# A mixer of grouped state space and attention: in each step VectorE serves the state-space pairs ahead of the projections' and heads' part

## What is computed

```
hn = rmsnorm(x)
u, c_q, c_kv, k_pe = split(hn @ w_in)             # 1024, 512, 256, 64 columns
y_ssm = s5_group(u)                               # state space, 64 groups of 16 inputs, 64 complex states
q = rmsnorm(c_q) @ w_uq ; kv = rmsnorm(c_kv) @ w_ukv
q_pe, k_pe = rope(q_pe), rope(k_pe)
y_mla = softmax(causal(q k^T)) v                  # 8 heads
h = x + concat(rmsnorm(y_ssm), rmsnorm(y_mla)) @ w_out
```

## Time and profile before

| | us |
|---|---|
| median of three executions | 2970.51 (2969.03 to 2972.24) |
| the profiled execution, its own time | 2971.62 |
| its span in the trace | 2969.8 |
| granted clock of TensorE, mean over the span | 0.988 |
| PE busy | 2865.9 (97%) |
| DVE busy | 2034.5 (69%) |
| POOL busy | 707.5 (24%) |

### The profile page before, as it was taken

How to read it: one execution, slowest core, us unless ns; L and a number is a source line. 1 busy time by engine, 2 the same in 40 slices (tenths; PEclk the granted TensorE clock), 3 DMA queues, 4 the chain that set the end, 5 groups by cost and what they waited for, 6 DMA issues and landing times.

```text
span 2969.8 us, 52389 instructions
## 1 busy us (share of the span) xinstructions
PE 2865.9 (97%) x21098; PEld 2545.0 (86%) x21098; DVE 2034.5 (69%) x3273; ACT 1552.8 (52%) x2574; POOL 707.5 (24%) x858
## 2 busy tenths in 40 slices
PE   8989999999999999899899999998999999999998
PEld 7868988888888888788788888997888888888887
DVE  6675887765777666677777766777676665566654
ACT  7345565544555555466556655465445444444443
POOL 0342211100121220766356630001021110011112
PEclk9999999999999999999999999999999999999999
DMA  6324555556555555322222223454555555655554
GB/s 247 103 70 146 183 189 194 184 176 208 186 197 181 177 183 206 114 90 93 79 94 93 104 94 121 153 185 151 173 184 193 190 186 174 208 190 193 181 180 149
DMA packets 79823, 475.40 MB, mean 160 GB/s; under 512 B 8224, under 2 KB 11296, under 8 KB 38304
## 3 DMA queue, kind: packets, MB, share of 16 engines
q1 hardware_dynamic: 76768, 459.72, 45.1%
q10 hardware_dynamic: 2816, 12.32, 1.2%
HBM read 465.72 MB, written 6.29 MB: 159 GB/s over the span
## 4 chain that ended last, share of the span: by engine, by line
PE 81%; DVE 10%; ACT 4%; issue 3%; POOL 2%; DMA 0%; SPq 0%; ACTq 0%; POOLq 0%; DVEq 0%
PE bank L764 36%; PE bank L768 23%; PE bank L766 5%; PE bank L767 5%; PE bank L757 3%; DVE m L1295 2%; ACT m L2182 2%; POOL m L2895 1%; POOL m L2891 1%; DVE m L1341 1%; PE bank L780 1%; PE bank L1097 1%; PE bank L1208 0%; PE bank L1101 0%; DVE m L1574 0%
## 5 line engine op out<-in xcount | busy, mean ns | idle before, releaser
L768 PE MATMUL bank<-m,m 128*128 128x256 f32 x6624 | 1860.4, 281 | 0.0
L764 PE MATMUL bank<-m,m 128*128 128x512 f32 x4736 | 1649.4, 393 | 6.9 <-DVE m L2056 5.7
L1295 DVE TENSOR_TENSOR m<-m,m 128x1024 fp32r<-128x1024 f32 (+1 forms) x912 | 1029.8, 1138 | 574.4 <-ACT m L2182 568.0
L768 PEld LDWEIGHTS bank<-m,m 128*128 128x128 f32 x6624 | 1252.4, 189 | 0.2
L2182 ACT ACTIVATE m<-m 128x1024 fp32r<-128x1024 f32 (+1 forms) x912 | 877.6, 976 | 650.6 <-PE bank L768 625.9
L764 PEld LDWEIGHTS bank<-m,m 128*128 128x128 f32 x4736 | 890.4, 188 | 206.4 <-DVE m L2056 5.9
L766 PE MATMUL bank<-m,m 128*128 128x256 f32 x1888 | 562.5, 298 | 28.9 <-DVE m L1295 24.9
L767 PE MATMUL bank<-m,m 128*128 128x256 f32 x1888 | 535.0, 283 | 0.0
L766 PEld LDWEIGHTS bank<-m,m 128*128 128x128 f32 x1888 | 362.0, 192 | 49.5 <-issue 39.1
L767 PEld LDWEIGHTS bank<-m,m 128*128 128x128 f32 x1888 | 362.6, 192 | 1.3
L2871 POOL TENSOR_TENSOR m<-m,m 128x256 fp32r<-128x256 f32 x44 | 63.5, 1442 | 547.7 <-ACT m L2472 547.7
(11 more groups left out here) (372 smaller groups left out, 2824.2 us busy)
## 6 DMA issues: line engine op xcount, KB each, us to landing
m<-in_w_up SPq DMA_DIRECT2D x88, 1024.0 KB, 4.8
m<-in_w_down SPq DMA_DIRECT2D x128, 704.0 KB, 4.1
m<-in_w_gu SPq DMA_DIRECT2D x88, 1024.0 KB, 4.8
m<-in_w_out SPq DMA_DIRECT2D x48, 1024.0 KB, 5.1
m<-in_w_krv SPq DMA_DIRECT2D x48, 1024.0 KB, 4.8
m<-in_w_xbc SPq DMA_DIRECT2D x24, 1024.0 KB, 4.8
m<-in_w_z SPq DMA_DIRECT2D x16, 1024.0 KB, 4.8
m<-in_w_in SPq DMA_DIRECT2D x14, 1024.0 KB, 6.2
```

The costliest lines, as they stand in the source:

```text
L764: pe.matmul(bank.rearrange("p (a b) -> p a b", a=2), hi, x, start=kc == L.k0, stop=False)
L768: m = pe.matmul(ps, lo, x[:, 0, :], start=False, stop=last)
L1295: v.tensor_tensor(lo_of(k), raw_of(k)[0], hi_of(k).bitcast(F32), SUB).then_inc(*lo_v(("lo", k)))
```

## The change

`first_mixer` gets a flag that puts the pairs ahead of `main` in the mix. Only VectorE's program sets it; PE, ACT, POOL and SyncE keep their order. No instruction is added, taken away or resized. All lines behind the first hunk are one further down.

```
-def first_mixer(main, setup, pair, tables, output):
+def first_mixer(main, setup, pair, tables, output, pairs_lead=False):
...
-    run(mix((main, 1), (pairs, 1), (ahead, 1), (outs, 1), (setup, 1)))
+    both = [(main, 1), (pairs, 1)]
+    run(mix(*(both[::-1] if pairs_lead else both), (ahead, 1), (outs, 1), (setup, 1)))
...
                               mix((flight(head, 16, 4), 1), (timed((GATES, spaced(linear(L_glu, glu)))), 1)),
-                              paired(mla_out())), setup(), s5_pair, s5_tables, s5_output)
+                              paired(mla_out())), setup(), s5_pair, s5_tables, s5_output, pairs_lead=True)
```

## The result

| | before | after |
|---|---|---|
| median | 2968.6 us (11 executions, 2966.81 to 2972.24) | 2976.7 us (11 executions, 2972.72 to 2984.24) |
| ratio, 95% interval | | 1.0024 [1.0016, 1.0032] |
| profiled execution, its own time | 2971.62 us | 2975.61 us |
| its span | 2969.8 us | 2973.8 us |
| mean granted clock | 0.988 | 0.989 |

The change makes the kernel slower by 0.24%, some 7 us (the medians themselves lie 8.1 us apart). The forecast was 2976.5 us.

What follows compares the result with a forecast made beforehand. PE was taken to bound 130 to 140 us, then mainly a ring through DVE and POOL to 208 us. Rounds' +4.7 and the clock's +1.3 make +6.0, on the median 2970.51 giving 2976.5 us; range 2971.0 to 2979.5.

Steps and rivals of the forecast that it cites:

- Free up to 140 us: Up to pair 7: evacuations up to 3 us later and the moved c_q norm rate (2.1 us) are covered, costing nothing.
- The new wait: Pairs 8, 13 and 14 wait for `y`, queued on PE behind `main`'s work; late `y` groups given chance 0.75.
- the rival in which `y` is in time: Rounds 7 to 8, 12 to 13, 13 to 14: no late `y`, leaving +1.0, 2971.5 us; chance 0.17.
- The ring's +4.7 us: Pairs 7 to 15: the loop through DVE and POOL, with late `y`, starts pair 15 4.7 us later.
- The round into pair 10: Rope 0 with its products before the scans and two L1323 behind them: priced at 9.01 us.
- S + 2.15: From the scans' end S: a rope or the second L1323 directly behind them is done 2.15 us later.
- Four L1323 behind the scans: Before pair 8: first gets in ahead of POOL's product; all four done 2.85 us after the scans' end.
- the low bound, S + 2.25: Before pair 8: low end for finishing four L1323, from a row beside three short POOL operations at 0.77 us each.
- The clock: PE's clock falls to half rate behind a wait before `y`; counted once, +1.3 us, on top of +4.7.
- The bound of +2.5 with all three falls: Upper bound for the clock's cost with falls at all three late places: 0.7 + 0.5 + 1.3 = 2.5 us.
- The range for the round into pair 14: Round from pair 13 to 14: near 10.5 us, up to 11.8; before the change 7.99.
- Nothing outside 140 to 210 us: The forecast would be wrong if anything outside this stretch of the kernel moved.

Runs made afterwards that it cites:

- run 6: The changed kernel with the pairs put ahead of the projections' part in PE's program too: 2967.92 us, 0.9992 of the kernel before.
- run 5: The changed kernel with unread matmuls filling PE's waits at three places, ahead of L_uq and of ropes 2 and 4: 2975.1 us, 1.0013 of the kernel before.
- run 4: The changed kernel with six unread matmuls on PE ahead of L_uq, filling one wait: 2975.78 us, 1.0023 of the kernel before.
- run 8: The kernel before with VectorE's product L1578 of each pair moved behind the next pair's two products: 2968.04 us, 0.9990 of the kernel before.
- run 3: The changed kernel with the chunks of c_q and ropes 1 to 4 back in their old slots: 2970.75 us, 0.9995 of the kernel before.
- Runs 1: The changed kernel with the four chunks of c_q and the evacuation of k_pe back at their old place: 2973.9 us, 1.0015 of the kernel before.

## Why the prediction was right, and where it was off

**Free up to 140 us: right.** Pair 7 started at 140.82 us (140.84 before); its wait shrank from 2.30 to 1.49 us. So 0.81 us of the cover were used and not the 2.1 of the forecast, with the same outcome.

**The new wait, `y` behind `main`'s work on PE: right, and shown.** Pairs 8, 13 and 14 wait for `y`; with PE's order changed (run 6) the waits are gone and the time is back. This also rules out the rival in which `y` is in time.

**The ring's +4.7 us: right.** The forecast's own terms add up to 4.8; run 5 gives 4.81 with one fall of the clock in it and 4.4 without. Its terms: into pair 8 9.57 us (9.6 forecast), into 9 7.21 (7.23), into 13 8.98 (8.92), into 14 10.45 (10.46), into 15 6.04 (6.05). The round into pair 10 was priced at 9.01 and took 8.56: in the kernel after the two L1324 behind the scans were done at S + 1.86 (167.66 against 165.80), not S + 2.15, and the gap before them took 5.78 us instead of 5.92. The round into 11, priced as bare, took 7.41; this is the fall of the clock at 168 us, which the forecast had nowhere. The 0.4 us of the one hides the 0.4 of the other, so that 4.8 against 4.8 is in part luck.

**Four L1323 behind the scans: a little dear.** From the end of the scans (145.54, where the next row starts, as the prediction counts S) they were done at 148.19, S + 2.65, priced at S + 2.85. The first gets in ahead of POOL's product as said, the second is done at S + 1.8 and not S + 2.15. The estimate from the Trainium skill's SBUF — State Buffer, by which the loser of the shared port pair blocks for the whole instruction, was S + 2.7 and came closer; the low bound, S + 2.25, for which the prediction gives no working, was too low. The round into pair 8 is met all the same, because PE had three blocks left to do behind the second chunk (1.56 us) and so it, not the last chunk, set the start of `y`. For the ropes the pattern of the earlier trace rows held: L1611 ended at 189.04, 0.28 us behind POOL's product. PE's waits were near the forecast for the ropes (2.22 and 2.45 us for 2.5 to 2.8); of the two of 2.5 us ahead of pair 8's `y` only the first came, the second was 0.64.

**The clock: the step that was mis-sized.** I wrote "I count it once, +1.3". Against run 5, with 6.98 for its round into pair 11, the first profile of the kernel after has 2.41 us more in the round into pair 8, 0.41 in 11, 0.37 in 13 and 0.06 in 14, 3.3 together; the second has 1.62, 1.59 and 2.48 more in 8, 13 and 14, 5.7 together. Less what the clock cost the kernel before (0 and 1.65), that is 3.3 and 4.0 us where the sum had 1.3. The count failed: three rounds had a price in each profile, not one. The place failed: I had the fall on L890 of rope 4, from the row in which I had seen one; in the first profile it came at 146, 172 and 192 us and not there, and the one at 172, behind PE's wait for L1568, was in no term. And the price failed: at 146 it slows not only what is left of the last tile (2.93 us for 1.56) but all of `y` (2.33 us from the first L875 to the end of L880, where run 4 took 1.29); the six prices run from 0.4 to 2.5 us. The bound of +2.5 with all three falls was too low as well: the second profile had all three, at 5.7. That all three waits would be followed by a fall came true in the second profile and not in the first.

That the predicted median is met to 0.2 us owes something to chance: the mixer lost 7.6 us in the first pair of profiles against the +6.0 forecast, and the medians lie 8.1 and 6.7 us apart; the median of the kernel before over all its executions was 1.9 us under that of its first three (2968.6 against 2970.51), from which the forecast was counted. The range for the round into pair 14, 10.5 to 11.8 us, held in the first profile (10.51) and not in the second (12.93).

**Nothing outside 140 to 210 us: right**, apart from a spread of the rest by some 5 us that both kernels have.

## What to carry to other kernels

Where two engines run the same mix of generators, an order is a contract between them. Changed on VectorE alone it cost 0.24%, on PE alone 0.98%, on both it gained 0.08% (an interval that ends at 1.0001): before one engine's order is changed, look what the other has queued behind the pieces that become late. Idle time of an engine pays only if nobody waits for what fills it; run 8, which shortens the ring itself, came out ahead of the kernel before (0.9990, an interval that ends at 0.9999), and run 3, which packs work into its gaps, did not clearly (0.9995). And where PE's clock can fall behind a wait, don't count on the filling of one: run 4 filled one and gained nothing in the median (1.0023), run 5 filled three (1.0013), and the clock still fell at a fourth.

## What the hardware showed

- **A fall of PE's clock isn't tied to a wait.** Idle for 2.81 us at 143 to 146 us, PE then ran at 0.50; idle for 2.45 us at 197 to 199.5, it stayed at 1.00; in the next profile of the same kernel the second wait had its fall too (0.50 in 200 to 202). Runs 1 and 4, in which PE has no long wait at 146 us, had a full clock there and falls at 186 and 196. The wait of 2.04 to 2.05 us for L1568 ahead of pair 11 had its fall in the first profile of the kernel after and in run 5, and none in the second of the kernel after. TensorE: Matmul & The Clock Gate in the Trainium skill says, in part 1, that the point at which the clock changes varies from run to run; the two profiles of one kernel agree.
- **What a fall costs is what stands directly behind it**: 1.37 us on six instructions of L758 and 1.04 on `y`, in the first profile. It costs the kernel nothing where no one waits, as in the kernel before at 192 us; in that kernel's second profile the fall at 152 us held up `y`, and the round into pair 9 took 9.00 us instead of 8.41.
- **Two-input operations of DVE beside POOL's**: L1611 took 1.38 to 1.39 us beside L2811 and 0.84 where it stood in the gap, four L1324 2.65 us beside one L2811 (and 3.08 beside three shorter ones).
- **The part behind the mixer, which no edit touches, differs by some 5 us between profiles** (2753.2 to 2758.9 us from `w_uv` on), which is more than most edits here are worth: a single profile can't rank them. Two profiles of one kernel lay closer (2758.1 and 2758.3, 2754.5 and 2753.2), and the cause is open.
